# A deeper ring of modulation loads in the head, a quarter of the shift and scale loads multiplied by TensorE there, and two places for the bias rows

## The reference

```
cond = jax.nn.silu(c)
for layer in range(DEPTH):                       # DEPTH = 2
    mod = cond @ w_ada[layer] + b_ada[layer]     # (1, 12288)
    sh_m, sc_m, g_m, sh_f, sc_f, g_f = jnp.split(mod[:, None, :], N_MOD, axis=-1)
    h = rms_norm(x, norm_mix_gain[layer]) * (1.0 + sc_m) + sh_m
    y = pool_mixer(h, ...) if layer == 0 else hgrn2_mixer(h, ...)
    x = x + g_m * y
    h = rms_norm(x, norm_ffn_gain[layer]) * (1.0 + sc_f) + sh_f
    x = x + g_f * swiglu(h, w_ffn_in[layer], w_ffn_out[layer])
return rms_norm(x, final_gain)
```

## Time and profile before

| | us |
|---|---|
| median of 3 runs | 2407.23 (2405.14 to 2408.24) |
| the profiled execution's own time | 2407.36 |
| its span, first to last instruction | 2405.6 |
| PE busy | 2139.1 (89%) |
| DVE busy | 1651.2 (69%) |
| ACT busy | 962.0 (40%) |
| DMA, mean over the span | 239 GB/s |

### The profile page before, as it was taken

One profiled execution on the slowest core, in us unless ns is written; L12 is line 12 of the kernel. 1 busy time (PEld: TensorE's weight loads), 2 busy tenths in 40 slices (PEclk: granted clock), 3 DMA queues, 4 the chain that ended last, 5 costly groups with the idle time before them and its releaser, 6 DMA issues. The chain is left out here.

```text
span 2405.6 us, 24936 instructions
## 1 busy us (share of the span) xinstructions
PE 2139.1 (89%) x9745; PEld 1750.7 (73%) x9745; DVE 1651.2 (69%) x1641; ACT 962.0 (40%) x1093; POOL 9.4 (0%) x43
## 2 busy tenths in 40 slices
PE   0173699999999999988989898898999999999997
PEld 0142588877778888877868776777888888888886
DVE  6878766768777667458878787886445447545744
ACT  2110344534344344444444444545434444443343
POOL 0000000000000000010000000000000000000000
PEclk9997799999999999999999999999999999999999
DMA  8878888867778888657767676574656668658764
GB/s 314 304 266 293 310 295 282 284 227 267 254 274 292 281 276 284 192 175 226 236 221 236 223 232 210 182 248 149 192 182 193 193 191 307 207 172 279 257 193 150
DMA packets 245893, 574.35 MB, mean 239 GB/s; under 512 B 17504, under 2 KB 17632, under 8 KB 245008
## 3 DMA queue, kind: packets, MB, share of 16 engines
q1 hardware_dynamic: 245776, 572.76, 71.5%
HBM read 570.59 MB, written 2.10 MB: 238 GB/s over the span
## 5 line engine op out<-in xcount | busy, mean ns | idle before, releaser
L980 DVE TENSOR_TENSOR w_lo<-raw,w_hi 128x1024 fp32r<-128x1024 f32 x696 | 845.2, 1223 | 526.0 <-ACT w_hi L674 524.9
L674 ACT ACTIVATE w_hi<-raw 128x1024 fp32r<-128x1024 f32 x696 | 722.0, 1057 | 665.6 <-PE prod L426 593.5
L424 PE MATMUL prod<-w_hi,h_hi 128*128 128x512 f32 x2080 | 832.5, 400 | 60.0 <-DVE w_lo L980 56.4
L426 PE MATMUL prod<-w_hi,h_lo 128*128 128x512 f32 x2080 | 815.8, 392 | 0.0
L425 PE MATMUL prod<-w_lo,h_hi 128*128 128x512 f32 x2080 | 815.2, 392 | 0.0
L424 PEld LDWEIGHTS prod<-w_hi,h_hi 128*128 128x128 f32 x2080 | 394.0, 189 | 162.7 <-DVE w_lo L980 73.5
L426 PEld LDWEIGHTS prod<-w_hi,h_lo 128*128 128x128 f32 x2080 | 393.5, 189 | 84.6
L425 PEld LDWEIGHTS prod<-w_lo,h_hi 128*128 128x128 f32 x2080 | 394.2, 189 | 79.0 <-issue 1.4
L1016 DVE SCALAR_TENSOR_TENSOR acc<-ada,cond,acc 128x1024 f32<-128x1024 f32 x292 | 373.5, 1279 | 9.9 <-DMA ada<-in_w_ada 6.8
L424 PE MATMUL prod<-w_hi,g_hi 128*128 128x512 f32 x704 | 275.1, 391 | 0.0
L426 PE MATMUL prod<-w_hi,g_lo 128*128 128x512 f32 x704 | 273.9, 389 | 0.0
(11 more groups left out here) (130 smaller groups left out, 900.2 us busy)
## 6 DMA issues: line engine op xcount, KB each, us to landing
ada<-in_w_ada SPq DMA_DIRECT2D x384, 512.0 KB, 5.3
raw<-in_w_ffn_in SPq DMA_DIRECT2D x352, 512.0 KB, 4.6
raw<-in_w_ffn_out SPq DMA_DIRECT2D x176, 512.0 KB, 4.5
raw<-in_hgrn_w_in SPq DMA_DIRECT2D x128, 512.0 KB, 4.0
raw<-in_hgrn_w_out SPq DMA_DIRECT2D x32, 512.0 KB, 4.7
raw<-in_pool_w SPq DMA_DIRECT2D x8, 512.0 KB, 7.3
xs<-in_x SPq DMA_DIRECT2D x2, 1024.0 KB, 8.9
out<-xs SPq DMA_DIRECT2D x2, 1024.0 KB, 3.9
```

The source lines that it names most:

```text
L424: pe.matmul(o, hi[:, k, ts], wh, start=(s == 0), stop=False)
L426: mm = pe.matmul(o, lo[:, k, ts], wh, start=False, stop=(s == n - 1))
L674: act.activation(w_hi[:, slot], raw[:, r], ACT.Copy).then_inc(hi_ready, 1)
L980: dve.tensor_tensor(w_lo[:, slot], raw[:, r], w_hi[:, slot], ALU.subtract).then_inc(lo_ready, 1)
```

## The change

The change touches only how units are loaded and folded:

- The head's pieces go through 16 buffers instead of 4. The 12 new ones (ada_head) lie in the pooling region. Units behind the head keep the four.
- Of each shift or scale unit of the head (0 to 3, 6 and 7) DVE folds 12 pieces instead of 16, and PE multiplies the last four (multiply_columns). That is eight matmuls a piece, each with a 128 x 128 block of the loaded piece as weights and one column of cond as the moving operand, added up in PSUM. Ahead of them stands one matmul with zeros over the eight columns (head_unit), which starts the sum, and behind them the eight matmuls that sum DVE's buffer, as before (sum_columns). The gate units keep 8 and 8.
- The bias rows have two places, partitions 0 and 32 for even units and 64 and 96 for odd ones, and SP waits for the unit before last.
- DVE's list in the head has fewer folds at each place: 88 where there were 112.

```
-    ADA = 4
-    PE_FOLDS = 8
+    ADA, ADA_HEAD = 4, 16
+    PE_FOLDS, PE_COLUMNS = 8, 4
...
+    def folded(u):
+
+        if u >= len(HEAD):
+            return 0, KD
+        return (PE_FOLDS, KD) if is_gate(u) else (0, KD - PE_COLUMNS)
+
+    def ada_slot(n):
+
+        head = len(HEAD) * KD
+        return (n % ADA_HEAD, n // ADA_HEAD) if n < head else (n % ADA, head // ADA_HEAD + (n - head) // ADA)
...
-        bias = sb("bias", [33, CH])
+        bias = sb("bias", [97, CH])
...
+            ada_head = sb("ada_head", [P, ADA_HEAD - ADA, UW], where=pooling)
...
-                    if u:
-                        sp.wait_ge(unit_summed, 2 * u)
+                    if u > 1:
+                        sp.wait_ge(unit_summed, 2 * (u - 1))
...
-                slot = n % ADA
-                if n >= ADA:
-                    sp.wait_ge(ada_free[slot], n // ADA)
-                sp.dma_start(ada[:, slot], w_ada[layer, k * P:(k + 1) * P, at:at + UW]).then_inc(ada_loaded[slot], 16)
+                slot, before = ada_slot(t.get("ada"))
+                if before:
+                    sp.wait_ge(ada_free[slot], before)
+                sp.dma_start(ada_buffer(slot), w_ada[layer, k * P:(k + 1) * P, at:at + UW]).then_inc(ada_loaded[slot], 16)
...
+            def multiply_columns(u, last):
+                for k in range(KD - PE_COLUMNS, KD):
+                    n = u * KD + k
+                    slot, _ = ada_slot(n)
+                    ada_arrived(pe, n)
+                    for j in range(UB):
+                        mm = pe.matmul(modp[:, 0, j:j + 1], ada_buffer(slot)[:, j * P:(j + 1) * P], cond[:, k:k + 1], start=False,
+                                       stop=(last and k == KD - 1 and j == UB - 1))
+                    mm.then_inc(ada_free[slot], 1)
+
+            def sum_columns(u, first, last):
+                pe.wait_ge(unit_summed, 2 * (u + 1))
+                a = unit_buffer(u)
+                for j in range(UB):
+                    mm = pe.matmul(modp[:, 0, j:j + 1], a[:, j * P:(j + 1) * P], ones[:, 0:1], start=first, stop=(first or (last and j == UB - 1)))
+                mm.then_inc(unit_reduced, 1)
+
+            def head_unit(u):
+
+                if u:
+                    pe.wait_ge(unit_taken, u)
+                pe.matmul(modp[:, 0, 0:UB], ones[:, :], zero[:, 0:UB], start=True, stop=False)
+                multiply_columns(u, False)
+                sum_columns(u, False, True)
...
-            reduce_unit(0)
+            pe.wait_ge(cond_ready, 1)
+            head_unit(0)
             turn_normalised()
-            reduce_unit(1)
+            head_unit(1)
             turn_normalised()
...
-            reduce_unit(6)
-            reduce_unit(7)
+            head_unit(6)
+            head_unit(7)
...
-            folds(4)
+            folds(3)
             pool_update(2)
             folds(2)
             pool_update(3)
-            folds(4)
+            folds(2)
             norm_root()
             folds(2)
             normalise(0)
-            folds(4)
-            folds(12)
+            folds(3)
+            folds(9)
```

More of the change, by code:

```diff
@@ L252, in multiplied, with ada_buffer, ada_arrived, ada_used @@
             eng.wait_ge(w_used, pairs_through(chunk))
+        def ada_buffer(slot):
+            return ada[:, slot] if slot < ADA else ada_head[:, slot - ADA]
+        def ada_arrived(eng, n):
+            slot, before = ada_slot(n)
+            eng.wait_ge(ada_loaded[slot], 16 * (before + 1))
+        def ada_used(eng, n):
+            slot, before = ada_slot(n)
+            eng.wait_ge(ada_free[slot], before + 1)
         def unit_buffer(u):
@@ L452, in reduce_unit @@
+            def reduce_unit(u):
+                if not is_gate(u):
+                    pe.wait_ge(unit_taken, u)
+                    sum_columns(u, True, True)
+                    return
+                a, begun = unit_buffer(u), u < len(HEAD)
                 pe.wait_ge(unit_summed, 2 * (u + 1))
-                if u and not begun:
+                if not begun:
                     pe.wait_ge(unit_taken, u)
[L455 to L460, removed]
+                for o in range(2):
+                    mm = pe.matmul(modp[:, o], ones[:, :], a[:, o * CH:(o + 1) * CH], start=not begun, stop=True)
@@ L1001, in fold @@
             def fold():
[L1002 to L1007, removed]
[L1008 to L1016 removed]
+                u = t.get("unit")
@@ new lines, in fold @@
+                first, last = folded(u)
+                k = first + t.get("folds")
+                n = u * KD + k
+                slot, _ = ada_slot(n)
+                a = unit_buffer(u)
+                if k == first and buffer_uses(u) > 0:
+                    dve.wait_ge(unit_reduced, buffer_uses(u))
+                ada_arrived(dve, n)
+                if k == first:
+                    ins = dve.tensor_scalar(a, ada_buffer(slot), cond[:, k:k + 1], None, ALU.mult)
+                else:
+                    ada_used(dve, n - 1)
+                    ins = dve.scalar_tensor_tensor(a, ada_buffer(slot), cond[:, k:k + 1], a, ALU.mult, ALU.add)
@@ L1017, in fold @@
                 ins.then_inc(ada_free[slot], 1)
[L1018 to L1021, removed]
+                t.tick("folds")
+                if k == last - 1:
+                    ada_used(dve, n)
+                    dve.wait_ge(bias_loaded[u % 2], 32 * (u // 2 + 1))
                     for r in range(2):
-                        b = a[32 * r:32 * r + 1, r * CH:(r + 1) * CH]
-                        dve.tensor_tensor(b, b, bias[32 * r:32 * r + 1, :], ALU.add).then_inc(unit_summed, 1)
+                        row = 64 * (u % 2) + 32 * r
+                        b = a[row:row + 1, r * CH:(r + 1) * CH]
+                        dve.tensor_tensor(b, b, bias[row:row + 1, :], ALU.add).then_inc(unit_summed, 1)
+                    t.tick("unit")
+                    t.n["folds"] = 0
```

43 lines of the change are left out of this document (20 added, 23 removed).

## The result

| | before | changed |
|---|---|---|
| median | 2407.72 us (2405.14 to 2408.24, 4 runs) | 2382.90 us (2378.06 to 2383.64, 4 runs) |
| the profiled execution's own time | 2407.36 | 2383.44 |
| its span | 2405.6 | 2381.7 |
| first FFN product | 266.94 | 242.02 |
| last copy of the head | 263.78 | 238.85 |

The ratio of the times is 0.9895, with a 95% interval of 0.9878 to 0.9912: the changed kernel is faster by 1.05%, or 24.8 us. The forecast was 2389, within its range of 2374 to 2402.

What follows compares the result with a forecast made beforehand. The prediction took PE to bound everything behind the first FFN product, so only the head could gain. Its terms, 6.9 + 1.3 + 3.1 + 5.4 + 1.4 = 18.1 us, took 2407.36 to 2389.3; forecast 2389, range 2374 to 2402.

Steps and rivals of the forecast that it cites:

- the last stretch: From the turn behind unit 5 to unit 7's copy: PE becomes the bound, 38.9 us for 40.3, -1.4.
- The chance of 0.61: Forecast's own case for the whole kernel: rates of 340 to 390 GB/s, blocks at 3.57 us, 2385 to 2396 us.
- up to unit 3's copy: Units 0 to 3: loads at 363 GB/s end unit 3, its copy at 123.5 for 130.36, -6.9 us.
- unit 4: Unit 4 of the head: DVE's list unchanged, only its wait for a piece goes, -1.3 us.
- unit 5: Unit 5 of the head: DVE loses 5.6 us of waits, PE ends the unit now, -3.1 us.
- unit 5's copy to the turn: Head, behind unit 5's copy: six folds for eight and one piece wait gone, 16.7 us for 22.1, -5.4.
- 358 GB/s: Loads up to unit 3: at this HBM limit the 13th piece lands 1.4 us later, sum 16.7 us.
- The bound of 0.86 beside the zeros: Starting matmul with zeros in each unit: between nothing and 0.86 us, the time of a 512-column matmul; taken as 0.45.
- Warm blocks: Head's column blocks: PE's clock rises to 2.4 GHz, a block costs 1.83 us; -34 us, time 2373, chance 0.18.
- The rate doesn't rise: Head's loads: deep ring leaves 309 GB/s, unit 3's copy at 137; -4 us, time 2403, chance 0.13.
- Slower PE blocks: Head's column blocks: weight loads can't overlap, 5.3 us a block instead of 3.57; time 2426, chance 0.08.

Runs made afterwards that it cites:

- the ring alone: Kernel before with a head ring of 16 buffers and two places for bias rows, no columns on PE: 2382.25 us, ratio 0.9895.
- the best one: Changed kernel, PE's pieces respread: none in units 0, 1; two in 2, 3; four in 6, ahead of the turn; three in 7: 2367.05 us.

## Why the prediction was right, and where its sizes were off

It was right in where the gain lies: all of it ahead of the first FFN product, with the rest of the kernel untouched, and in the last stretch PE takes over from DVE. It was wrong in what bounds units 0 to 3, where half of the gain is made: it had the loads end unit 3, and the trace shows DVE there. The total still fell into the range because that error is 6 us in a range of 28. The chance of 0.61 was for rates of 340 to 390 GB/s and for 2385 to 2396 us, and neither came: the 36.2 MB up to that piece were there by 96.1, which is 398 GB/s or more.

| step | forecast | measured |
|---|---|---|
| up to unit 3's copy | -6.9 | -13.0 |
| unit 4 | -1.3 | -1.9 |
| unit 5 | -3.1 | -1.4 |
| unit 5's copy to the turn | -5.4 | -5.6 |
| the turn to unit 7's copy | -1.4 | -3.1 |
| sum | -18.1 | -24.9 |

**The step that was off is the first.** I took the loads as the bound of units 0 to 3, at 363 GB/s, with the 13th piece of unit 3 at 104.8. From 20 to 80 us they run at 410 to 419 in windows of 20 us; with 410 the same sum gives 5.1 + 36.2 MB / 410 = 93.4. PE starts those blocks at 96.1 without a wait. What ends the unit then is DVE, whose bias rows end at 113.7, and PE has stood 3.83 us for it. DVE in turn had stood 10.6 us for unit 1's copy at 70.43, behind PE's blocks. My rate came from stretches of the kernel before in which four buffers or the products behind the head set the demand, and I read what was asked for as what could be had. It is the share of 1.00 beside it that misled me: 372 GB/s at 1.00, and 410 at 1.03 here. The trace of before had more to say. Rows 3 has 399 GB/s over 3.7 us, and ten of the fifteen microseconds that I read as 372 are this row of the windows view:

```profile
90.00:100.00 10.00, 3.57 (x16) 3.49 (x16) 4.68 (x5) 3.13 (x7) 0.00 (x0) 1.00 1.03 396
```

The other evidence that I left out are DVE's waits for pieces ahead of unit 3's copy, 16.9 us by 130 us. They bound how much a deeper ring can give there; the ring alone brought unit 3's copy 14.3 us earlier (116.11 for 130.36).

On that step the forecast also weighed the Trainium skill's 358 GB/s (DMA: Bandwidth & Descriptors, Where 436 GB/s comes from) as a second value. The trace speaks against it as a bound for this one core: 381 over 120 us, 419 over 20. The Trainium skill (HBM Reference, Specifications (TRN2)) says that a core that streams alone gets well above that share, about 425 GB/s, and the trace agrees.

**Unit 5** gained less. Its step is PE's, as forecast, but the first 16 records of multiply_loads took 9.19 where 14.06 / 2 = 7.03 had been taken. The changed kernel with the ring of 8 has 7.13 there, after the same 3.78 us of a cold sum and the same 1.11 of idle time:

```profile
164.47 7.13 PE L467 MATMUL modp<-ada,cond_rows 128*128 128x512 f32 x16 [1.11 <-ACT gate L746]
```

The granted clock is 0.62 from 156 to 162 us in the changed kernel, and 1.00 from 164.4 to 171.6 in that one, so this is the clock. Why it rises earlier in one than in the other is open, and so no difference of 2 us between two of these kernels should be read as the effect of their edit.

**The last stretch** took 37.2 us for 38.9. Unit 6 costs 17.5 (203.40 to the end of its sum at 220.89) and unit 7 17.65, not 18.3: four blocks in a row take 13.65 until the next record instead of four times the 3.57 that a block alone shows, the zeros 0.29 in unit 6 and not 0.45, and the turn 1.76 until the next record and not 2.0. These are small things that were all taken too large. (The bound of 0.86 beside the zeros should read 0.88, 14.06 us for 16 matmuls; nothing hangs on it.)

**About 1 us is given back** behind the head: the product comes 24.9 earlier and the span ends 23.9 earlier. The first products run slow until 245.9, 3.9 us, as against 2.7 before, which at half the speed makes 0.6 of it; the rest is not followed up.

**The rivals.** Warm blocks: out, by 0.50 over 200 to 240 us, and in the first 120 us, where the clock column says 1.00, by the same 13.79 for four blocks. The rate doesn't rise: out, by 410 to 419 from 20 to 80 us (the 381 for 309 over 120 us has loads in it that run ahead). Slower PE blocks: out, by 3.45. That the ring alone would do it was not among them, and the prediction counted the columns as a trade that it didn't price apart. The experiments show that in this form the columns are worth nothing beside the ring of 16, cost 17 us in a ring of eight (2397.3 against 2380.1) and 30 us in a ring of four (2438.0 against 2407.8).

## What to carry to other kernels

Work that is moved from one engine to another is worth what the receiving engine has idle at that place in the chain: over the ring alone the columns gained nothing while unit 6's four blocks stood behind a turn, and 8 us once those were moved ahead of it (6.6 by the first products in the traces). Count a buffer that a slow consumer holds as lost to the ring; the depth that a ring needs is set by the pieces held, and a small load in the same queue with a wait of its own can undo that depth. And read a transfer rate as a capacity only where nothing but the transfers themselves could have set it.

## What the runs showed of the hardware that was not expected

- Loads of 512 KB by one queue ran at 410 to 419 GB/s over 20 us in the kernels with 16 buffers, and at 398 over the first 120 us in the best one. Sixteen are not needed for the rate itself: the ring alone with 8 buffers shows 422 and 418 GB/s in 20 to 40 and 40 to 60 us. With four the mean was 309, and still 10 us of that kernel, 162 to 172, ran at 410.
- A PE that is busy 18.4 us of 20 with one-column float32 matmuls stays at a granted clock of 0.50, and so does one that is busy 44.7 of 45 with 512-column products among them. The FFN's products that follow (fp32r, one record each 0.427 us and then 0.227) run at the higher level from 245.9 us on (granted clock 1.00 from 246 to 250).
- A float32 matmul of 512 columns takes 0.88 us in a row in the pool stage (7.03 for eight) and 1.84 among the column blocks, at the lower level.
